# Moving the rounding of the next weight tile ahead of the convolution tap, and its residue behind the taps, in the first feed-forward part of a two-layer kernel

## The reference

```
h = rms_norm(x, g_pre_ffn)
u = causal_depthwise_conv(h @ w_up, conv_w, conv_b)      # w_up: 1024 x 5632, three taps along the tokens
gate, val = jnp.split(u, 2, axis=-1)
f = (jax.nn.gelu(gate, approximate=True) * val) @ w_down  # w_down: 2816 x 1024
x = x + rms_norm(f, g_post_ffn)
```

## Time and profile before

| | |
|---|---|
| time, three runs | 1007.25 us median (1006.81 to 1019.7) |
| profiled execution | 1007.77 us, of which the span is 1006.0 us |
| TensorE busy | 907.8 us, 90% of the span |
| VectorE busy | 678.2 us, 67% |
| ScalarE busy | 509.2 us, 51% |
| GpSimd busy | 318.1 us, 32% |
| mean granted clock of TensorE | 0.938 of full speed |

### The profile page before, as it was taken

The page is one execution under the profiler, slowest core; times in us unless marked ns, Lnnn a source line. Parts: engine busy times, 40 slices in busy tenths (PEclk is TensorE's granted clock), DMA queues, the critical chain, the costliest instruction groups (busy, mean ns, idle before and its releaser), DMA issues.

```text
span 1006.0 us, 16923 instructions
## 1 busy us (share of the span) xinstructions
PE 907.8 (90%) x6718; PEld 861.8 (86%) x6718; DVE 678.2 (67%) x984; ACT 509.2 (51%) x926; POOL 318.1 (32%) x150
## 2 busy tenths in 40 slices
PE   4996879998879897988999788999998899999998
PEld 3985769998879886977889678988898899999998
DVE  7857742877666766276779998783668466566573
ACT  5477345743444445665664554255544454444440
POOL 3653103111221212423455751121243222222220
PEclk8997779999999999899999989799899899999999
DMA  5734005344445455534346361222154355666651
GB/s 181 272 114 139 21 2 158 116 135 127 147 143 168 138 162 163 171 103 129 127 157 186 106 228 45 83 82 88 63 147 147 126 156 180 189 189 182 183 161 43
DMA packets 54078, 137.18 MB, mean 136 GB/s; under 512 B 6000, under 2 KB 24816, under 8 KB 53872
## 3 DMA queue, kind: packets, MB, share of 16 engines
q1 hardware_dynamic: 54000, 136.11, 43.3%
HBM read 135.03 MB, written 1.05 MB: 135 GB/s over the span
## 4 chain that ended last, share of the span: by engine, by line
PE 62%; DVE 20%; ACT 9%; issue 8%; DMA 1%; DVEq 0%; SPq 0%; ACTq 0%
PE PROD L576 11%; PE PROD L577 11%; PE PROD L578 11%; ACT whi L1012 5%; DVE wlo L1491 4%; DVE YC L1774 3%; PE SC L717 3%; PE OP L761 3%; PE PROD L638 2%; DVE RS L1499 2%; PE SC L576 2%; PE TP L578 2%; PE TP L577 2%; PE TP L576 2%; PE SC L577 2%
## 5 line engine op out<-in xcount | busy, mean ns | idle before, releaser
L559 POOL TENSOR_TENSOR wlo<-raw,whi 128x1024 fp32r<-128x1024 f32 x124 | 314.3, 2542 | 664.3 <-ACT whi L1012 664.3
L576 PE MATMUL PROD<-HA,whi 128*128 128x256 f32 x1096 | 320.9, 293 | 22.8 <-DVE HA L1519 7.1
L577 PE MATMUL PROD<-HA,wlo 128*128 128x256 f32 x1096 | 316.2, 288 | 0.0
L578 PE MATMUL PROD<-HA,whi 128*128 128x256 f32 x1096 | 315.9, 288 | 0.0
L1491 DVE TENSOR_TENSOR wlo<-raw,whi 128x1024 fp32r<-128x1024 f32 x128 | 185.5, 1453 | 153.0 <-ACT whi L1012 152.8
L1012 ACT ACTIVATE whi<-raw 128x1024 fp32r<-128x1024 f32 x252 | 261.9, 1050 | 44.9 <-PE PROD L578 23.9
L576 PEld LDWEIGHTS PROD<-HA,whi 128*128 128x128 f32 x1096 | 216.8, 198 | 26.3 <-DVE HA L1519 7.9
L577 PEld LDWEIGHTS PROD<-HA,wlo 128*128 128x128 f32 x1096 | 217.0, 198 | 0.6 <-issue 0.5
L578 PEld LDWEIGHTS PROD<-HA,whi 128*128 128x128 f32 x1096 | 216.5, 198 | 0.0
L1905 DVE SCALAR_TENSOR_TENSOR CY<-U,CV,CY 128x255 f32<-128x255 f32 (+29 forms) x120 | 67.3, 633 | 0.2
L576 PE MATMUL SC<-ACTS,whi 128*128 128x256 f32 x176 | 52.8, 300 | 16.2 <-DVE ACTS L1519 8.1
(11 more groups left out here) (316 smaller groups left out, 1761.0 us busy)
## 6 DMA issues: line engine op xcount, KB each, us to landing
raw<-stream SPq DMA_DIRECT2D x208, 512.0 KB, 3.8
raw<-stream SPq DMA_DIRECT2D x136, 128.0 KB, 2.4
raw<-stream SPq DMA_DIRECT2D x8, 384.0 KB, 3.2
raw<-stream SPq DMA_DIRECT2D x8, 256.0 KB, 3.1
X<-xT SPq DMA_DIRECT2D x2, 512.0 KB, 5.0
E<-memT SPq DMA_DIRECT2D x1, 1024.0 KB, 5.8
out<-X SPq DMA_DIRECT2D x8, 128.0 KB, 2.0
PX<-pT SPq DMA_DIRECT2D x1, 256.0 KB, 3.8
```

The costliest lines, as they stand in the source:

```text
L559: nc.gpsimd.tensor_tensor(wlo[:, n % NSPLIT, :], raw[:, n % NRAW, :], whi[:, n % NSPLIT, :].bitcast(F32), ALU.subtract).then_inc(lo_pool, 1)
L576: nc.tensor.matmul(dst, wh, hi, start=start, stop=False, skip_group_check=True)
L577: nc.tensor.matmul(dst, wl, hi, start=False, stop=False, skip_group_check=True)
L578: last = nc.tensor.matmul(dst, wh, lo, start=False, stop=stop, skip_group_check=True)
```

## The change

On ScalarE, `conv_first` calls `ahead(o)` at its start in place of its end: the rounding of the next tile is issued ahead of the wait for the scaled output and of the tap. On VectorE, `ahead(o)` is taken out of `up_scaled`. The loop over the steps now calls it for output 2j after the taps and the product of the step before (in a flushed step directly after `up_scaled(j, 0)`, since there those are done), and for output 2j + 1 after `conv_rest(j, 0)`. No instruction is added or taken away; the second FFN and all other stages are as they were.

```
@@ conv_first(j, g) on ScalarE
                 o = ("up", 2 * j + g)
+                ahead(o)
                 wait_freed(act, o)
                 if j >= 2:
                     act.wait_ge(act_out, j - 1)
                 ch = g * FC + j
                 nc.scalar.activation(YC[:, j % 2, g, :], UU[:, j % 2, g, :], ACT.Identity, ...
-                ahead(o)

@@ the loop over the steps on VectorE
                 if j and not flushed:
                     conv_rest(j - 1, 1)
                     act_mul(j - 1)
+                ahead(("up", 2 * j))
                 up_scaled(j, 1)
                 if j and not flushed:
                     low(ACTS, "a", j - 1, G1[:, (j - 1) % 2, 1, :])
                 conv_rest(j, 0)
+                ahead(("up", 2 * j + 1))
                 if j % 2 and j // 2 in DOWN_AFTER:
                     conv_rest(j, 1)
```

## The result

The changed kernel takes 975.5 us (median of 4 runs, 972.8 to 987.0) against 1009.3 us for the kernel before in the same comparison. The ratio is 0.9694 with a 95% interval of 0.9648 to 0.9740: 3% faster. The profiled execution took 972.8 us, its span is 971.1 us, 34.9 us shorter than the span of before.

A forecast was written before the change was run, and what follows sets the result against it. The prediction took VectorE's list in the first FFN as the bound: 210.7 us, less 52.4 of waits, plus 20.2 from GpSimd, gives 178.5. That is 32.2 us less, about 976 us for the kernel, range 966 to 998.

The forecast's parts named there:

- Which engine bounds: First FFN: VectorE's own list, 210.7 us, is the path, because its scalings never wait for TensorE's product.
- The residues' waits: First FFN: VectorE's residues wait 60.4 us for ScalarE's rounding; the change removes 52.4 us, and 7.5 stay at flushed ends.
- The holds: First FFN: VectorE instructions held while GpSimd subtracts, 2.0 us for each of 15 GpSimd residues; 20.2 us given back.
- The sum: VectorE's list in the first FFN: 210.7 - 52.4 + 20.2 = 178.5 us, 32.2 us less, so 975.6 us for the profiled execution.
- The tap behind a rounding: ScalarE's tap comes up to 1.04 us later behind the rounding; VectorE's two taps have slack, so cost 0.
- The DMAs: SyncE's refills of `raw` come 0.9 to 2 us later but stay hidden; cost 0, DMA share under 0.6.
- The period: Six tiles of the first FFN, 20.85 us before, would take 17 to 18 us in the changed profile.
- TensorE as the bound: Rival: GpSimd holds VectorE only 0.8 us each as before, so TensorE's blocks decide the first FFN; 969 us, chance 0.14.
- The partial case: Rival: VectorE still catches ScalarE amid a rounding, 0.7 us in about 22 steps, 15 us back; 991 us, chance 0.22.
- The case of no effect: Rival: residues find roundings as late as before, since something else holds ScalarE in front; 1007 us, chance 0.10.
- The slower rival: Rival: ScalarE's rounding waits for TensorE ahead of the tap, 0.62 us in each of 44 outputs; 1034 us, chance 0.06.

## Why the prediction was right

**Which engine bounds.** That VectorE's list was the path rested on scalings that never wait for a product. The list got 33.9 us shorter, the end of the stage came 33.4 us earlier, and the span got 34.9 us shorter. The difference between the first and the last is: 0.7 us, by which the list began earlier, 1.1 us more between its end and TensorE's, and 1.5 us less behind the stage, where nothing was changed.

How near TensorE already is to being the bound is seen in its own rows: the stage before, then two stretches of the changed kernel, and the waits that the prediction left out, before and then after:

```profile
188.30:422.00 233.70, 204.63 (x1595) 200.77 (x1594) 151.68 (x230) 112.46 (x176) 55.78 (x24) 0.94 0.50 150
```

```profile
249.30:366.10 116.80, 116.71 (x969) 116.11 (x967) 105.94 (x151) 68.59 (x103) 35.76 (x14) 1.00 0.63 192
368.90:375.70 6.80, 5.82 (x27) 5.82 (x28) 2.98 (x5) 5.29 (x10) 2.47 (x1) 0.50 0.52 160
```

```profile
PE SC L576 <- POOL wlo L559: 7.3, 3, 3.4
...
PE PROD L576 <- POOL wlo L559: 3.6, 2, 1.9
```

```profile
PE SC L576 <- POOL wlo L559: 1.0, 1, 1.0
```

The prediction read TensorE's waits as waits for VectorE. It overlooked 11.7 us for GpSimd's residues (these two lines and one of 0.8 us), more than the 7.0 us for a bank. VectorE's scalings never waited for TensorE all the same, so the sum did not suffer. In all TensorE stood still for 29.1 us of the stage before and for 4.8 us in the changed one, and its busy time there fell by 8.8 us (204.63 to 195.87). In the changed kernel it stands still for 1.0 us at 248 us and then not until 366.1, and VectorE works off what it is behind: its scalings start 10.5 us after TensorE's last matmul for the output at the 13th output, 7.2 us at the 24th and 6.2 us at the 44th. What is left of that is paid once, at the end: TensorE waits 3.8 us, up to 369.9, for the last activation's residue, and from 368.9 to 375.7 its granted clock is 0.50 (1.2 GHz). So the prediction's view, that VectorE decides the end and TensorE by itself would be some 11 us earlier, held (with no residue on GpSimd TensorE ends at 377.8 in place of 388.2); but in most of the stage neither engine held the other up.

**The residues' waits.** Forecast 52.4 us removed; measured 59.9 - 7.8 = 52.1. Seven of the eight that stay, 7.4 us of them, are at the flushed ends, as was said.

**The holds.** Forecast from 15 to 35.2 us; measured 33.2. This term was the least certain, with bounds from 0.8 to 2.4 us a residue of GpSimd. The measured mean is 1.75; I had 2.0 for 15 of them and 1.3 for four. Exactly 19 instructions are long: 5 residues with 1.4 us of excess each, 13 taps with 1.9 and one product with 2.0. Without this term the forecast would have been 955 us, and TensorE's end would have cut it to 969. The Trainium skill's rule in SBUF — State Buffer, "SBUF: two separate sides", that such instructions exclude each other, agrees with these traces for taps, products, residues and the scalings that were not held. Its worst case, 2.4 us for each, was not reached.

**The sum.** 210.7 - 52.1 + 18.2 = 176.8 us, the measured list, against 178.5 forecast. That it closes to the last digit is chance: the new waits of 1.4 and 0.7 us are not in it, and with them it closes to 2 us. 1.7 of the 2.8 us between the profiled execution's 972.8 and the forecast's 975.6 are the list; the other 1.1 are the terms of 0.7, 1.1 and 1.5 us above. That the median, 975.5, lies half a microsecond from the forecast is chance too, with runs from 972.8 to 987.0; the shortening of the profiled execution, 34.9 us against 32.2, is the fairer measure.

**The tap behind a rounding.** Forecast 0; VectorE's taps waited 0.7 us in two cases.

**The DMAs.** Forecast 0 and a share under 0.6; the share is 0.58 and no rounding waited for a tile.

**The period.** I said 17 to 18 us for six tiles, and it was 16.75. That is less than TensorE's own 17.3; VectorE falls behind TensorE in the two steps with `head_norm` (its reciprocals take 3.35 us each) and catches up afterwards, as its delays of 10.5, 7.2 and 6.2 us above show.

**The rivals.** TensorE as the bound is real, but lies behind the holds: it took all residues off GpSimd to come to it. The partial case didn't happen with both halves; with each half alone a part of the waits stays, 30.1 and 24.7 us. The case of no effect fell with the waits, from 59.9 to 7.8 us. The slower rival failed in its mechanism, not only in its condition: its waits appeared with one bank, 65 us of them, and the changed order was 30 us faster all the same. The prediction charged 0.62 us an output for a later tap as if the tap were in line with the next scaling, and it is beside it.

The version with the changed order and all residues of the first FFN on VectorE, at 964.0 us, beats both kernels.

## What to carry to other kernels

In an engine's fixed list, what costs is not that a producer is slow but that its result is asked for directly after the request. Let the producer start on the condition that it really has, ahead of work that waits for the consumer, and let the consumer do its other work first; half of this gives more than half of the gain.

Before waits are removed, look at what they cover: idle time of VectorE hid GpSimd's subtractions, and with the idle time gone these cost more than they spared. An assignment of work that paid in the old order has to be weighed anew in the new one: here GpSimd's share was worth 22 us of list before the change and cost 9 after it.

## What the runs showed of the hardware that was not expected

How much of GpSimd's instruction a VectorE instruction waits out is shown by 19 and 29 of them in one stage: 1.75 and 1.86 us of the 2.4 to 2.7 they take. GpSimd's own also get longer where VectorE is dense, 2.40 us on average before, 2.53 in the changed kernel and 2.75 with half of the residues, so it seems that the engine that comes second waits, on both sides. Scalings, which read PSUM, are free of it: 14 of them start within a subtraction of GpSimd, at least 0.3 us before its end, in the kernel with half of the residues there, and each takes 0.41 or 0.42 us.

With two PSUM banks for the up outputs in place of four the changed kernel's list is 1.5 us longer, and with one it is 32.5 us longer: a second bank is worth nearly everything here, a third and fourth nearly nothing.
